# Products of constants in front of TensorE's waits, at the stage borders of a two-layer mixer block

## What is computed

```python
for l in range(DEPTH):                          # DEPTH = 2
    last = l == DEPTH - 1
    mod = silu(c) @ w_ada[l] + b_ada[l]         # shifts, scales and gates, also for the context
    y, yc = hybrid_mixer(x * (1 + sc1) + sh1, ctx * (1 + csc1) + csh1, ...)
    x = layer_norm(ALPHA * x + g1 * y, ln1_g[l], ln1_b[l])
    x = layer_norm(ALPHA * x + g2 * swiglu(x * (1 + sc2) + sh2, w_gu[l], w_down[l]), ln2_g[l], ln2_b[l])
    if not last:
        ...                                     # the same for ctx

def hybrid_mixer(h, hc, ...):
    aq, ak, av, bq, bk, bv, z, xbc, dt = split_projection(h @ w_in)
    out_a = window_sink_attention(rope(aq), rope(ak), av, ...)
    out_b = global_block_attention(rope(rms_norm(bq)), rope(rms_norm(bk)), bv, ...)
    out_c = ssd_output(bidir_ssd(...), ...)     # a two-way state-space scan
    return concatenate([out_a, out_b, out_c]) @ w_out
```

## Time and profile before

| | |
|---|---|
| median of 3 runs | 3463.29 us |
| the profiled execution | 3464.08 us |
| its span, first to last instruction | 3462.3 us |
| TensorE busy | 3258.0 us, 94% of the span |
| VectorE, ScalarE, GpSimd busy | 1803.3, 1003.8, 1370.6 us |
| mean granted TensorE clock | 0.973 of full speed |

### The profile page before, as it was taken

One profiled execution on the slowest core, in us unless ns is written; L12 is line 12 of the kernel. 1 busy time (PEld: TensorE's weight loads), 2 busy tenths in 40 slices (PEclk: granted clock), 3 DMA queues, 4 the chain that ended last, 5 costly groups with the idle time before them and its releaser, 6 DMA issues. The chain is left out here.

```text
span 3462.3 us, 44540 instructions
## 1 busy us (share of the span) xinstructions
PE 3258.0 (94%) x16996; PEld 2738.3 (79%) x16996; DVE 1803.3 (52%) x2906; ACT 1003.8 (29%) x2022; POOL 1370.6 (40%) x1001
## 2 busy tenths in 40 slices
PE   4979989999999999999998979989899999999997
PEld 4768878778788888888886759878677788888886
DVE  8377958695673333333235867926686511211224
ACT  5257742361430000000003347732342300000003
POOL 0154213354434344344434353222344454454454
PEclk9979999999999999999999979999999999999999
DMA  8200023003111212111111600020022111111111
GB/s 330 74 1 1 1 106 101 21 25 122 55 50 67 67 67 69 64 61 61 42 37 68 244 18 1 1 67 31 16 77 85 49 55 48 42 55 48 42 52 52
DMA packets 69809, 214.13 MB, mean 62 GB/s; under 512 B 6816, under 2 KB 19104, under 8 KB 68256
## 3 DMA queue, kind: packets, MB, share of 16 engines
q1 hardware_dynamic: 62224, 183.86, 15.4%
q10 hardware_dynamic: 7440, 28.34, 2.3%
HBM read 192.78 MB, written 19.40 MB: 61 GB/s over the span
## 5 line engine op out<-in xcount | busy, mean ns | idle before, releaser
L205 PE MATMUL ps<-h_hi,f_whi 128*128 128x512 f32 (+1 forms) x1760 | 651.0, 370 | 3.5 <-DVE f_gated L3276 3.5
L206 PE MATMUL ps<-h_lo,f_whi 128*128 128x512 f32 (+1 forms) x1760 | 649.3, 369 | 0.0
L207 PE MATMUL ps<-h_hi,f_wlo 128*128 128x512 f32 (+1 forms) x1760 | 648.9, 369 | 0.0
L3276 DVE TENSOR_TENSOR f_gated<-f_gated,ps 128x512 f32<-128x512 f32 (+1 forms) x110 | 69.7, 634 | 812.5 <-PE ps L207 811.2
L3090 POOL TENSOR_TENSOR f_whi<-f_wraw,small 128x1024 fp32r<-128x1024 f32 x130 | 247.6, 1904 | 556.4 <-PE ps L207 529.6
L3287 DVE SCALAR_TENSOR_TENSOR x_res<-ps,mod,x_res 128x512 f32<-128x512 f32 (+1 forms) x448 | 308.5, 689 | 245.1 <-PE ps L207 243.9
L205 PEld LDWEIGHTS ps<-h_hi,f_whi 128*128 128x128 f32 x1760 | 332.5, 189 | 60.9 <-DVE f_gated L3276 3.9
L206 PEld LDWEIGHTS ps<-h_lo,f_whi 128*128 128x128 f32 x1760 | 332.4, 189 | 55.7 <-issue 1.0
L207 PEld LDWEIGHTS ps<-h_hi,f_wlo 128*128 128x128 f32 x1760 | 332.4, 189 | 55.2
L205 PE MATMUL ps<-f_ahi,f_whi 128*128 128x512 f32 (+1 forms) x896 | 337.9, 377 | 0.5 <-DVE x_res L3287 0.5
L3092 POOL TENSOR_TENSOR f_wlo<-f_wraw,f_whi 128x1024 fp32r<-128x1024 f32 x130 | 327.0, 2515 | 10.2
(11 more groups left out here) (299 smaller groups left out, 6452.4 us busy)
## 6 DMA issues: line engine op xcount, KB each, us to landing
f_wraw<-in_w_ffn SPq DMA_DIRECT2D x130, 512.0 KB, 3.2
ada_w<-in_w_ada SPq DMA_DIRECT2D x80, 512.0 KB, 5.3
later_w<-in_w_ada ACTq DMA_DIRECT2D x32, 512.0 KB, 3.2
o_wraw<-in_w_out SPq DMA_DIRECT2D x28, 512.0 KB, 3.3
wrawc<-in_w_in SPq DMA_DIRECT2D x26, 512.0 KB, 4.3
wrawab<-in_w_in SPq DMA_DIRECT2D x16, 512.0 KB, 6.3
x_res<-x_spill SPq DMA_DIRECT2D x6, 1024.0 KB, 8.7
x_res<-in_xT SPq DMA_DIRECT2D x8, 640.0 KB, 7.4
```

What stands on the lines that cost most here:

```text
L205: pe.matmul(out, w_hi, h_hi, start=first, stop=False)
L206: pe.matmul(out, w_hi, h_lo, start=False, stop=False)
L207: return pe.matmul(out, w_lo, h_hi, start=False, stop=last)
L3276: dve.tensor_tensor(g, g, pl.bank(3 + c, tn), ALU.mult).then_inc(u_taken[c], 1)
```

## The change

A helper issues n products of two constants, the 128x128 matrix of ones and the first 512 columns of the table of constants, both plain float32, into a PSUM bank that nothing reads before it is written again. Calls to it are put at eight places of TensorE's programs: at the start of norm_and_rotate, before its turn 3 of the second group and at its end; at the start of project_ssd, scan, project_out and feed_forward; and in NextNorm, behind a wait for weights and ahead of the first block. Both layers pass all of them but NextNorm, which only layer 0 has. Layer 0 gets 2+4+7+6+2+2+1+5 = 29 products, layer 1 2+4+5+6+2+2+1 = 22. Nothing is removed, and nothing moves on another engine. The pieces of the diff are, in order: the helper; norm_and_rotate's turn, start and end; project_ssd; scan; project_out; NextNorm; feed_forward.

```diff
+def hold_clock(pl, pe, bank, n):
+    for _ in range(n):
+        pe.matmul(pl.bank(bank), pl.c(ONES), pl.const[:, 0:512], start=True, stop=True)
...
                 if m == 0:
                     pe.wait_ge(rot_ready, 1)
+                if m == 3:
+                    hold_clock(pl, pe, 7, 4)
                 if m >= 2:
                     pe.wait_ge(with_sin[1], m - 1)
...
+            hold_clock(pl, pe, 7, 2)
             b = 0
             for n in range(N):
...
             for m in range(b, len(turns_b)):
                 rotate_b(m)
+            hold_clock(pl, pe, 7, 5 if last else 7)
...
             pe.sem_inc(full[1], 2)
+            hold_clock(pl, pe, 7, 6)
...
         def _(pe):
+            hold_clock(pl, pe, 5, 2)
+
             def backward(o):
...
+            hold_clock(pl, pe, 7, 2)
             for n in range(plain + 4):
                 turn(0, n)
...
         pe.wait_ge(nxt.ring.ready, 4)
+        hold_clock(pl, pe, 5, 5)
         self.block(pe, 0, 0)
...
+            hold_clock(pl, pe, 7, 1)
             norm.mean(pe, 1)
```

More of the change, by code:

```diff
@@ L2648, in tensor @@
     def tensor(self, pe):
-        nxt = self.next
+        pl, nxt = self.pl, self.next
         pe.sem_inc(nxt.full[1], 2)
```

## The result

The kernel with the change took 3471.20 us (median of 20 runs, 3466.09 to 3477.77); the kernel before, beside it, 3464.03 us (20 runs, 3461.32 to 3466.40). The ratio is 1.0022, with a 95% interval of 1.0015 to 1.0028: slower by 7.2 us, where 1.3 more was predicted. The profiled execution took 3469.0 us, its span is 3467.2 us.

What follows compares the result with a forecast made beforehand. It took TensorE, busy 94% of the span, and its granted clock as the bound. Terms 0.7 - 2.9 - 0.8 + 3.0 + 0 + 1.25 = +1.25 us gave 3465.3 profiled, 3464.6 us as median; range 3457.5 to 3471.

Steps and rivals of the forecast that it cites:

- The price of a product: Any place: one product of 512 plain float32 columns takes 0.86 us at 2.4 GHz and 1.70 at 1.2 GHz.
- project_ssd was forecast at -2.9: Start of project_ssd: six products in the 6.1 us wait let it open at full clock, -1.4 and -1.5 us by layer.
- GpSimd's wait of 6.86 us: Sign expected in the profile, late in layer 0's norm_and_rotate: this wait on ScalarE's copy becomes about 4 us.
- the gain of turn 3: Four products in the 4.7 us wait ahead of turn 3: -3.1 us in layer 0 if the clock is kept, 0 in layer 1.
- Rival (a): Attention's opening: the clock is kept into it, -3.5 us a layer, 3457.6 us in all; chance 0.14.
- Rival (c): Turn 3: products cost as forecast but the turn keeps nothing, no -3.1 in layer 0, 3467.7 us; chance 0.2.
- Rival (d): Whole kernel: waits swallow all products and no clock changes, 3463.3 us; chance 0.1.
- Rival (b): All openings: products stay on the path at half clock, +23 us at most, 3475 with half; chance 0.16.
- norm_and_rotate together: 2.2 - 3.1 + 1.6 = +0.7: norm_and_rotate: start products +2.2 in layer 0 and +1.6 in layer 1, turn 3 -3.1 in layer 0.
- two products take 1.7, so the first real one is 0.3 late ... Sum -0.8: Start of scan: two products nearly fit the 1.4 us behind the barrier; -0.9 us in layer 0, +0.1 in layer 1.
- denser work should raise the clock earlier and give most back: +0.7: Start of project_out, layer 1: two uncovered products cost +0.7 us after give-back; layer 0 +2.3, sum +3.0.
- feed_forward, +0.7 in layer 1: feed_forward's start: one product, partly covered by 0.36 us, costs +0.55 and +0.7 us, +1.25 in all.

Runs made afterwards that it cites:

- experiment 3: The changed kernel with all product counts 0 except the 6 at the start of project_ssd: 3462.08 us, ratio 0.9995 to the kernel before.
- experiment 9: The changed kernel with only the 4 products ahead of turn 3 and the 6 at project_ssd's start: 3459.22 us against 3465.01 before, ratio 0.9984.
- experiment 2: The changed kernel with only the products in long waits (turn 3, norm_and_rotate's end, project_ssd, NextNorm): 3461.27 us, ratio 0.9988 to the kernel before.
- the first experiment: The changed kernel with only the products right behind barriers (starts of norm_and_rotate, scan, project_out, feed_forward): 3479.14 us against 3464.29 before, ratio 1.0047.
- its repetition: The changed kernel measured and profiled once more, nothing altered: 3474.22 us against 3465.01 for the kernel before, ratio 1.0024.
- experiment 12: The changed kernel with only norm_and_rotate's 2 products at its start and 4 ahead of turn 3: 3466.89 us against 3465.42 before, ratio 1.0006.
- experiment 10: The changed kernel with only the 2 products at the start of scan: 3464.06 us, ratio 0.9997 to the kernel before.
- experiments 8: The changed kernel with all product counts 0 except the 4 ahead of turn 3: 3464.12 us, ratio 0.9997 to the kernel before.
- experiment 7: Only project_out's opening products, 4 instead of the change's 2: 3472.57 us, ratio 1.0024 to the kernel before.
- experiment 5: The change's calls emptied; products put ahead of barriers instead, at the ends of projections, project_ssd, scan and project_out: 3468.57 us against 3464.68 before, ratio 1.0009.
- experiments 1, 4, 5, 6, 7, 8 and 12: Of these, 6 has no line elsewhere: the whole change with products of 2 columns instead of 512, 3467.06 us, ratio 1.0009 to the kernel before.
- experiment 4: Only the products at norm_and_rotate's end, 12 and 9 instead of the change's 7 and 5: 3466.22 us, ratio 1.0008 to the kernel before.

## Why the prediction was wrong

**What held.** The price of a product (0.86 and 1.70 us) and the reading of the waits held. project_ssd was forecast at -2.9 and had -3.05 and -3.04 in the change; that close a hit is luck in part, since alone (experiment 3) it had -2.03, with the turn -2.23, and layer 0's stage was up to 1.05 shorter without any product. That scan behind it would take part of the gain back (+0.55 and +0.93 in experiment 3) stood in no term. The turn alone had -2.94 for -3.1, though there the four left no idleness over which the clock had to be kept; where they left it, the stage had -2.90 (experiment 9) and only -1.60 (experiment 2). Project_out's and norm_and_rotate's costs in single stages (+2.3 for +2.48; +2.2 for the +2.27 of the first experiment) were right in layer 0. Of the signs, GpSimd's wait of 6.86 us became 5.76 and not about 4, for the gain of turn 3 did not arrive. Rival (a) fell: no hold of the change kept the clock into attention, and the fourth experiment shows that it would not have paid. Rival (c) fell as it was put, for the turn alone kept its gain; in the change it came true by another way, as the first step below tells. Rival (d) fell. Rival (b) was right in kind, a third of its way: products that run at half clock behind a barrier stay on the path, in norm_and_rotate, scan and project_out.

**The failing steps.** Four terms of the sum were wrong, and all in one direction:

1. "norm_and_rotate together: 2.2 - 3.1 + 1.6 = +0.7". The two prices of layer 0 were each right and could not be added. The start's products use up the cover that the turn's were laid into. The change had +0.52, its repetition +1.34, and with nothing but these two calls +0.51, for -0.9. Layer 1's share gave less back than forecast: its first sum was 3.1 us late, and the stage took +2.31 and +2.60 for +1.6 (+2.37 in the first experiment). In total 2.1 and 3.2 us were missed. For layer 0 experiment 12 shows it; why layer 1 gives back so little is not shown.
2. "two products take 1.7, so the first real one is 0.3 late ... Sum -0.8" for scan. It supposed the full clock at the barrier, where it was in the kernel before. In the change the clock was at half there in layer 0, in both profiles, so that the products took up to 3.5 us and the first real one was 3.60 (repeated 3.24) behind the barrier instead of 1.43. The start of the products behind was 2.28 and 1.03 us later. In experiment 10, at full clock, they cost nothing (-0.37 and +0.10), and experiment 3 shows that the half clock at this border goes with the products of project_ssd. The rest of layer 0's +4.47 lies in the stage's last products, half clock from 782.9 on; experiments 8 and 12, with no product in scan, had +1.95 and +2.14 in the same way, so that part need not be the change's.
3. "denser work should raise the clock earlier and give most back: +0.7" for project_out in layer 1. It had +2.35, +2.54 and, in the first experiment, +2.20; layer 0 had 0.2 more than its +2.3. The clock did rise earlier, at +6.0 us instead of +9.2, and the first product with weights was 1.25 late, for 3.55 put in front; nearly twice the +0.7. Another 1.1 us went behind a wait of 5.66 us late in the stage, where half clock reaches further over dense work than before; this was not foreseen, and what sets its end is open. Windows from that wait's end to the clock's rise, in the kernel before and then after:

```profile
2675.40:2679.05 3.65, 3.65 (x9) 2.88 (x10) 3.65 (x6) 2.45 (x4) 0.00 (x0) 0.50 0.00 0
2678.14:2684.17 6.03, 6.03 (x14) 4.76 (x15) 6.03 (x10) 2.71 (x4) 0.00 (x0) 0.50 0.00 0
```

4. feed_forward, +0.7 in layer 1, had +1.11 and +1.10: the term was right in kind and 0.4 short.

By the smaller difference of the two profiles the four stages, both layers together, come to 2.1 + 3.1 + 1.8 + 0.4 = 7.4 us, where the measured difference (7.2) lies 5.9 above the forecast's (1.3). Of scan's 3.1, 0.8 lies behind its opening in layer 0, where profiles differ without the change.

**A rule weighed in the prediction.** The Trainium skill ("TensorE: Matmul & The Clock Gate", Part 4) has transposes not count as activity, by which two real products in front of them would be worth their time. In experiment 7 four products stand in front of the transposes, in experiment 5 three stand ahead of the barrier: the transposes then take 2.8 us instead of 5.4, and layer 0's stage is longer in both. In the kernel before the clock rose in layer 0 when only transposes had run since the barrier. So no run here bears out a gain by that rule. Layer 1 decides nothing: the clock rose there 9.2 us behind the barrier without the two products and 6.0 with them, which the rule and the denser work of the prediction both allow, and the stage was longer all the same.

**What stays open.** Why the clock goes to half ahead of scan's opening with project_ssd's products and behind it, or not at all, without them: the gap ahead of the barrier is as long in both. And why in layer 0's scan the clock fell 5.2 to 9.4 us ahead of the stage's end in nine of the fourteen profiles (the change, its repetition, and experiments 1, 4, 5, 6, 7, 8 and 12) and less than 1 us ahead of it in the other five, that before among them. In layer 0, NextNorm's and feed_forward's share (-1.44 and +0.92) can't be told from chance; experiment 2, with NextNorm's five products and not feed_forward's, had -0.46, the ninth, with neither, -0.30, and the eighth, with neither, +2.69. No run shows a cost of NextNorm's products.

## What to carry to other kernels

In this kernel, products that keep the clock up paid only inside a wait that is longer than they are, with dense work of TensorE's own at once behind it: turn 3 (4.7 us of wait) gained 1.6 to 2.9 us in layer 0, and project_ssd (6.1 us of wait, then products without a gap) 1.1 to 1.2 us in layer 1 and 0.8 to 2.1 in layer 0, of which scan behind it gave 0.5 to 1.2 a layer back where it had no products of its own. Products right behind a barrier whose first real product was ready cost up to 2.5 us a stage. Behind a gap that has lost the clock they run at half clock themselves (two of them took 3.5 us, and 1.8 where the clock was up), so price them by the clock at that place, and try both prices where the row doesn't fix it. Don't add the prices of two places in one stage before looking whether the first delays the arrival at the second and takes its cover. Before moving the clock into a stage, look whether its opening is paced by other engines: attention, warmed, waited more and lost the clock later, over denser work. And look at the stage behind the one that gains.

## What the runs showed of the hardware

- A clock brought up ahead of a border fell in the midst of the opening that followed: at +6.6 and +6.2 us in attention (experiment 4), at +5.1 in project_out (experiment 5). Before, the same openings were at half from the start and rose once.
- How long attention's opening stays at half clock, with the same instructions, went with 2 to 3 us of the stage: until 19.8 us behind the barrier with +2.6, until 14.0 with -0.63, against until 16.0 before.
- The part ahead of the first stage border has no product of the change and took 164.84 to 168.58 us over the change's two profiles; one profile can't show a difference of a few us in a total, and stage lengths need several.
- Two columns instead of 512 took most of the cost away in project_out (+0.37 instead of +2.48) and in norm_and_rotate, not in feed_forward (+1.77 in layer 1, with +1.11 for 512 columns).
- The same 1.3 us of idleness ahead of turn 3, behind products at full clock, went with a kept clock in one kernel (experiment 9) and with a fall 1.7 us behind it in another (experiment 2).
